# Retention: a head's group statistics used one chunk later, and its transposes released head by head

## What is computed

```python
def head_groupnorm(o):                       # over the 512 channels of a head
    mu = jnp.mean(o, axis=-1, keepdims=True)
    var = jnp.mean(jnp.square(o - mu), axis=-1, keepdims=True)
    return (o - mu) * lax.rsqrt(var + GN_EPS)

q, k, v, z_ret, u_val, u_gate, z_conv, g_a, g_b = jnp.split(h @ w_in, split_at, axis=-1)
ret = head_groupnorm(retention_chunkwise(rotary(q), rotary(k), v))   # 4 heads, 512 value channels each
y_a = (ret * jax.nn.silu(z_ret)) @ w_ret_out

a = u_val * jax.nn.sigmoid(u_gate)
a = causal_depthwise_conv_2(a, conv_w, conv_b)                       # 31 taps, 1024 channels
a = jax.nn.silu(layernorm(a))
y_b = (a * jax.nn.silu(z_conv)) @ w_conv_out
merged = jax.nn.sigmoid(g_a) * y_a + jax.nn.sigmoid(g_b) * y_b
```

## Time and profile before

| | |
|---|---|
| Median of 3 runs | 933.23 us (931.78 to 934.69) |
| Profiled execution | 932.75 us, its span 930.7 us |
| PE busy | 887.7 us |
| DVE busy | 693.0 us |
| ACT busy | 509.9 us |
| POOL busy | 46.1 us |
| HBM read | 156.58 MB |

### The profile page before, as it was taken

How to read it: one execution, slowest core, us unless ns; L and a number is a source line. 1 busy time by engine, 2 the same in 40 slices (tenths; PEclk the granted TensorE clock), 3 DMA queues, 4 the chain that set the end, 5 groups by cost and what they waited for, 6 DMA issues and landing times.

```text
span 930.7 us, 16363 instructions
## 1 busy us (share of the span) xinstructions
PE 887.7 (95%) x6434; PEld 826.9 (89%) x6434; DVE 693.0 (74%) x1116; ACT 509.9 (55%) x728; POOL 46.1 (5%) x48
## 2 busy tenths in 40 slices
PE   5898998989989899999999999999999989999997
PEld 5898997879867899999998889999887779999995
DVE  4676887944765767777777677899998879965874
ACT  4587884645444555556555555433345566445642
POOL 0001120012110000000000000000001130001000
PEclk9899998988999799999999979999999999999999
DMA  7825564540068257777778616555554435654441
GB/s 215 262 88 162 172 191 138 172 96 2 27 217 298 78 192 246 261 250 252 249 244 303 211 57 204 181 182 181 167 175 155 137 121 174 203 183 156 144 153 46
DMA packets 139475, 161.58 MB, mean 174 GB/s; under 512 B 17155, under 2 KB 112283, under 8 KB 139419
## 3 DMA queue, kind: packets, MB, share of 16 engines
q1 hardware_dynamic: 139419, 160.80, 53.2%
HBM read 156.58 MB, written 4.21 MB: 173 GB/s over the span
## 4 chain that ended last, share of the span: by engine, by line
PE 76%; DVE 12%; ACT 7%; issue 2%; DMA 2%; SPq 0%; DVEq 0%; ACTq 0%
PE psum L480 22%; PE psum L482 22%; PE psum L481 22%; DVE w_lo L1374 5%; PE psum L765 3%; DVE cv L1817 2%; ACT w_hi L933 2%; DMA w_raw<-in_sc_w_out_dram 1%; DVE cacc L1523 1%; PE psum L635 1%; ACT junk L966 1%; PE psum L869 1%; PE psum L747 1%; PE psum L647 1%; PE psum L604 1%
## 5 line engine op out<-in xcount | busy, mean ns | idle before, releaser
L1374 DVE TENSOR_TENSOR w_lo<-w_raw,w_hi 128x1024 fp32r<-128x1024 f32 x264 | 321.4, 1241 | 151.0 <-ACT w_hi L933 149.9
L933 ACT ACTIVATE w_hi<-w_raw 128x1024 fp32r<-128x1024 f32 x264 | 274.2, 1057 | 223.3 <-PE psum L482 171.5
L480 PE MATMUL psum<-hT_hi,w_hi 128*128 128x256 f32 x1216 | 349.6, 287 | 4.7 <-DVE w_lo L1374 4.0
L481 PE MATMUL psum<-hT_lo,w_hi 128*128 128x256 f32 x1216 | 346.6, 285 | 0.0
L482 PE MATMUL psum<-hT_hi,w_lo 128*128 128x256 f32 x1216 | 346.5, 285 | 0.0
L480 PEld LDWEIGHTS psum<-hT_hi,w_hi 128*128 128x128 f32 x1216 | 236.3, 194 | 6.2 <-issue 4.3
L481 PEld LDWEIGHTS psum<-hT_lo,w_hi 128*128 128x128 f32 x1216 | 236.2, 194 | 0.3 <-issue 0.2
L482 PEld LDWEIGHTS psum<-hT_hi,w_lo 128*128 128x128 f32 x1216 | 235.9, 194 | 0.0
L1817 DVE SCALAR_TENSOR_TENSOR cv<-aP,par,cv 128x256 f32<-128x256 f32 x240 | 98.5, 479 | 0.0
L480 PE MATMUL psum<-w_hi,hT_hi 128*128 128x512 f32 x224 | 92.7, 414 | 2.3 <-DVE w_lo L1374 2.3
L482 PE MATMUL psum<-w_hi,hT_lo 128*128 128x512 f32 x224 | 88.8, 396 | 0.0
(11 more groups left out here) (283 smaller groups left out, 1073.8 us busy)
## 6 DMA issues: line engine op xcount, KB each, us to landing
w_raw<-in_w_in_dram SPq DMA_DIRECT2D x44, 1024.0 KB, 5.0
w_raw<-in_sc_w_in_dram SPq DMA_DIRECT2D x32, 1024.0 KB, 7.5
w_raw<-in_gdn_w_in_dram SPq DMA_DIRECT2D x24, 1024.0 KB, 5.4
ada<-in_w_ada_dram SPq DMA_DIRECT2D x24, 512.0 KB, 4.7
w_raw<-in_gdn_w_out_dram SPq DMA_DIRECT2D x8, 1024.0 KB, 5.2
w_raw<-in_sc_w_out_dram SPq DMA_DIRECT2D x8, 1024.0 KB, 8.0
w_raw<-in_w_ret_out_dram SPq DMA_DIRECT2D x8, 1024.0 KB, 4.9
w_raw<-in_w_conv_out_dram SPq DMA_DIRECT2D x4, 1024.0 KB, 5.0
```

What stands on the lines that cost most here:

```text
L480: pe.matmul(o, l_hi, r_hi, start=start, stop=False, skip_group_check=True)
L481: pe.matmul(o, l_hi, r_lo, start=False, stop=False, skip_group_check=True)
L933: act.activation(w_hi[j % 2 * 2 + h][:, :, :], raw[slot][:, h * KH2:(h + 1) * KH2, :], ACT.Copy).then_inc(hi_ready, 1)
L1374: return dve.tensor_tensor(o, whole, hi.bitcast(F32), ALU.subtract)
```

## The change

ACT and DVE take the square root, reciprocal and scaling of head h out of the odd chunk 2h + 1 and do them at the next chunk, behind its splits: ACT before that chunk's Silu, DVE before its convolution steps. Head 3's stands in zconv chunk 0. PE's block of transposes for pairs 2c and 2c + 1 stands beside zconv chunk c (before: c + 1), waits only for the products of its own head, and for the sums that are still in the banks it writes. ACT's and DVE's yT_hi and yT_lo move with it; ACT's waits for the product that reads the part of `zr` that it overwrites.

```diff
@@ PE
             def turn_two(c):
                 for kp in (2 * c, 2 * c + 1):
-                    if kp == 0:
-                        pe.wait_ge(rg_ready, NT * RH)
+                    pe.wait_ge(rg_ready, NT * (kp // 2 + 1))
+                    pe.wait_ge(gn_ready, min(kp + 5, NT * RH))
                     if kp >= 4:
                         pe.wait_ge(y_op_ready, 2 * KT + kp - 3)
...
-            phase("zconv", hT_hi, hT_lo, True, beside=lambda c: turn_two(c - 1) if c else None)
-
-            phase("gates", hT_hi, hT_lo, True, beside=lambda c: turn_two(KT // 2 - 1) if c == 0 else None)
+            phase("zconv", hT_hi, hT_lo, True, beside=turn_two)
+            phase("gates", hT_hi, hT_lo, True)
@@ ACT
-            def group_norm(i, j, done):
+            def group_norm(h):
+                act.wait_ge(gn_step, 2 * NT * (h + 1))
+                if h:
+                    act.wait_ge(gn_ready, NT * h)
+                act.activation(grs[:, :], gmv[:, :, 1], ACT.Sqrt, bias=eps_n[:, :]).then_inc(gn_std, 1)
+                act.wait_ge(gn_rec, 2 * (h + 1))
+                for t in range(NT):
+                    n = NT * h + t
+                    if h:
+                        act.wait_ge(rg_ready, n - 1)
+                    act.activation(og[t][:, :], psum[:, 4 + n % 4, :], ACT.Identity, scale=grs[:, t:t + 1], bias=gnm[:, t:t + 1]).then_inc(gn_ready, 1)
+
+            def beside_zret(i, j, done):
+                c = 4 * i + j
+                if c and c % 2 == 0:
+                    group_norm(c // 2 - 1)
                 z_ret(i, j, done)
-                if j % NT == NT - 1:
-                    h = (4 * i + j) // NT
...
             def turned_pairs(i, j, done):
+                if j == 0:
+                    group_norm(RH - 1)
                 z_conv(i, j, done)
-                if j == 1:
-                    act.wait_ge(rg_ready, NT * RH)
-                if j:
-                    split_two(j - 1)
+                split_two(j)
 
             def split_two(q):
                 for kp in (2 * q, 2 * q + 1):
+                    if kp < NT * RH // 2:
+                        act.wait_ge(rg_ready, NT * kp + 1)
                     act.wait_ge(yT_turned, KT + kp + 1)
...
-            def last_pairs(i, j, done):
-                gates(i, j, done)
-                if i == 0 and j == 0:
-                    split_two(KT // 2 - 1)
-            chunks("gates", last_pairs, unroll=True)
+            chunks("gates", gates, unroll=True)
@@ DVE
+            def group_scale(h):
+                dve.wait_ge(gn_std, h + 1)
+                dve.reciprocal(grs[:, :], grs[:, :]).then_inc(gn_rec, 1)
+                dve.wait_ge(gn_rec, 2 * h + 1)
+                dve.scalar_tensor_tensor(out=gnm[:, :], in0=gmv[:, :, 0], scalar=-1.0, in1=grs[:, :], op0=ALU.mult, op1=ALU.mult).then_inc(gn_rec, 1)
+
             def group_norm(i, j, done):
                 n = 4 * i + j
                 h, t = n // NT, n % NT
+                if n and t == 0:
+                    group_scale(h - 1)
                 conv_share(7)
...
-                if t == NT - 1:
-                    dve.wait_ge(gn_std, h + 1)
-                    dve.reciprocal(grs[:, :], grs[:, :]).then_inc(gn_rec, 1)
...
             def turned_pairs(i, j, done):
+                if j == 0:
+                    group_scale(RH - 1)
                 conv_share(5 if j else 8)
-                if j:
-                    split_two(j - 1)
+                split_two(j)
...
                 conv_share(8 if c else 4)
-                if c == 0:
-                    split_two(KT // 2 - 1)
```

More of the change, by code:

```diff
@@ L1245, in _ @@
             z_ret = tokens_out(zr, ACT.Silu)
-            def group_norm(i, j, done):
-                z_ret(i, j, done)
-                if j % NT == NT - 1:
-                    h = (4 * i + j) // NT
[L1251 to L1261, removed]
+            def group_norm(h):
[13 more added lines that the diff above has]
+                    group_norm(c // 2 - 1)
+                z_ret(i, j, done)
+            chunks("zret", beside_zret, unroll=True)
             z_conv = channels_out(zc, ACT.Silu)
             def turned_pairs(i, j, done):
+                if j == 0:
+                    group_norm(RH - 1)
                 z_conv(i, j, done)
-                if j == 1:
-                    act.wait_ge(rg_ready, NT * RH)
-                if j:
-                    split_two(j - 1)
+                split_two(j)
             def split_two(q):
                 for kp in (2 * q, 2 * q + 1):
+                    if kp < NT * RH // 2:
+                        act.wait_ge(rg_ready, NT * kp + 1)
                     act.wait_ge(yT_turned, KT + kp + 1)
@@ L1882, in group_norm @@
                 dve.bn_aggr(gmv[:, t, :], gst[:, t, :]).then_inc(gn_step, 1)
-                if t == NT - 1:
-                    dve.wait_ge(gn_std, h + 1)
-                    dve.reciprocal(grs[:, :], grs[:, :]).then_inc(gn_rec, 1)
-                    dve.wait_ge(gn_rec, 2 * h + 1)
-                    dve.scalar_tensor_tensor(out=gnm[:, :], in0=gmv[:, :, 0], scalar=-1.0, in1=grs[:, :], op0=ALU.mult, op1=ALU.mult).then_inc(gn_rec, 1)
             chunks("zret", group_norm, unroll=True)
             def turned_pairs(i, j, done):
+                if j == 0:
+                    group_scale(RH - 1)
                 conv_share(5 if j else 8)
-                if j:
-                    split_two(j - 1)
+                split_two(j)
             def split_two(q):
```

## The result

The changed kernel takes 926.19 us (median of 6 runs, 923.88 to 928.74) against 933.28 us (6 runs of before): ratio 0.9923, 95% interval 0.9904 to 0.9942, so 5.4 to 9.0 us faster. The profiled execution took 926.39 us, with a span of 924.4.

What follows compares the result with a forecast made beforehand. PE, busy 95% of the span, bounds the kernel; only its stops and low clock can return. 6.4 us less 2.1 gives 4.3 off 932.75, so 928.45, plus 0.5 for the median: 928.9, stated as 928.8; range 926.3 to 931.2.

Steps and rivals of the forecast that it cites:

- What could be won: Zret to first gates chunk: four PE stops cost 4.7 us, the clock's fall 1.7; at most 6.4 us can return.
- The circle of waits undone: Zret: ACT and DVE no longer wait for each other once per head; without holds DVE's period falls from 15.8 to 12.1 us.
- no stop in zret: Sign of being right: PE runs through the retention gate without a stop; three of four stops go.
- A convolution step held like w_lo: DVE convolution steps beside POOL's products are held about 1.1 us each, two per head; DVE's period becomes 14.3 us.
- the first rival: Convolution steps not held by POOL: DVE never falls behind, all 6.4 us come, 926.8 us; chance 0.15.
- One stop of about 2 us stands where four were, and costs 2.1 us: Zconv, third chunk's second half: PE waits for a DVE split ready at 768.4 but wanted at 766.2.
- the 4.3 of the sum: Whole kernel: net gain in us, 6.4 to be won less 2.1 for the stop left.
- The transposes earlier save nothing: Zconv: same 32 transposes, 8 yT_hi and 8 yT_lo, moved forward, so no PE work saved; added PE waits cost nothing.
- the clock did not fall after the stop: Rival: the clock falls in the remaining stop, PE loses 1.7 us more, 930.5 us; chance 0.15.
- the holds were not longer: Rival: holds of 1.3 us each, ten before the zconv split, make the stop 4 us; 930.9 us, chance 0.12.
- nothing was slower: Rival: steps held again behind the next POOL product, ten holds of 1.1 + e; at e = 1.0 938.9 us; chance 0.04.
- The clock: After the 1.91 us stop PE fell from 2.4 to 1.2 GHz for a while, worth 1.7 us.

Runs made afterwards that it cites:

- stats_only: The changed kernel with transposes, yT_hi and yT_lo put back where they were before, only the group statistics a chunk later; ratio to before 0.9925.
- before_again: The kernel before the change, once more with no edit, timed beside itself: 932.88 against 933.26 us.
- pool_twice: The changed kernel with every POOL gate product made twice, the first time into a free buffer; ratio to before 1.0053.

## Why the prediction was right or wrong

- **What could be won**: 6.4 us. The stage without any stop is 127.0 us, so before held 133.4 - 127.0 = 6.4. Right; on one of its terms see the last point.
- **The circle of waits undone; no stop in zret; the clock at 1.0 there**: right. DVE's waits went as said, and its first convolution block starts 14.07 us after the first weighted sum (714.59 - 700.52); from 715.5 and before's 701.48 the forecast had 14.0.
- **A convolution step held like w_lo**: right in kind, and it decided against the first rival. The hold was put at 1.1 us; it is 1.04. DVE's period was put at 14.3 us; it is 14.03 (714.59, 728.62, 742.65).
- **"One stop of about 2 us stands where four were, and costs 2.1 us"**: this is the step that was mis-sized. The stop is at the chunk named, for the split named, but 0.78 us long, and costs 128.1 - 127.0 = 1.1. So 1.0 us more came back than the 4.3 of the sum. DVE was put too late: three periods too long by 0.27 make 0.8 us, and the 8 steps with four holds, put at 7.6, took 763.82 - 756.68 = 7.1. About half of these 1.3 us is the price of the hold, 1.1 in place of 1.04 or less, ten times. The other half is DVE's own work: its period without holds was put at 12.1 and is 14.03 - 2.09 = 11.94. The sum took DVE's waits at their idle time alone. In before, the product that follows the reciprocal (gnm) and the next w_lo start 2.62 us apart, with the wait of 2.46 between them,

```profile
728.05 0.16 DVE L1887 SCALAR_TENSOR_TENSOR gnm<-gmv,grs 128x2 f32<-128x2 f32 x1
730.67 3.19 DVE L1374 TENSOR_TENSOR w_lo<-w_raw,w_hi 128x1024 fp32r<-128x1024 f32 x2 [2.46 <-ACT w_hi L933]
```

and in the changed kernel, without a wait, gnm and the next instruction start 0.08 apart (714.51, 714.59): 2.54 us were lost, not 2.46. All of it adds up because DVE is the late engine over the whole way from 714 to 767.
- **The transposes earlier save nothing and put 1.2 us of yT_lo and a block of 0.8 into the first zconv chunk**: right; stats_only shows 0.3 us lost. That the waits of PE on POOL and ACT cost nothing was right too: L895 has none.
- **A slip that changed nothing**: the time at which PE wants the second zconv chunk's split, 759.8, leaves out that stop's own 1.1 us and the 0.79 of the transposes; with both it is 759.5, and DVE's 756.9 is early all the same.
- **The rivals**: the clock did not fall after the stop (1.00 from 754 to 795); the holds were not longer; nothing was slower.
- **The range**: its lower end was the gain without any stop, 6.4 us, from a median. Between two comparisons of the same pair of kernels the difference of the medians was 7.1 and 5.1 us; of the 7.1 one microsecond is in front of the stage in the two profiles, and where the rest arose is not shown. The stage alone, 5.3 us, would have given 927.9, inside the range: that the time fell 0.1 us outside took the mis-sized stop and the scatter together. The range took in the bounds of the costs and forgot that of the measurement, about 2 us.
- **The clock**: as an account of PE's time the 1.7 us are right. As the price of the fall they are wrong: without the fall PE would have waited instead, as before_again shows below.

## What to carry to other kernels

If two in-order engines wait for each other once per round, move the use of the result one round later, behind the work that the other engine is waiting for; here this gave 5.6 us, and letting the consumers start earlier gave nothing. But look first at what ran in the idle time that goes: there POOL's two products of a head had cost DVE 0.85 us together (w_lo x2 at 3.18 in the earlier trace rows against 2.33 without POOL), and as soon as they met DVE's convolution steps they cost 1.04 us each for 1.3 us of POOL. Where one price stands in a sum ten times, its second digit matters, and so does the 0.1 us that a wait costs beyond its idle.

## What was not expected

- **A fall of the clock can be free.** In before_again PE stopped for 1.95 us at the same place as in before, and the clock did not fall after it. PE then ran ahead at full rate, and its next stop was 2.42 us instead of 0.84. The restart came 764.03 - 701.15 = 62.9 us after the first weighted sum, in before 764.41 - 701.48 = 62.9. DVE set that moment: its w_lo for it starts 60.8 us after the mark in both (761.95 - 701.15 and 762.29 - 701.48). PE at half rate merely filled the wait. Afterwards the clock fell after the longer stop, where PE could less well afford it, and the stage was 0.6 us longer. Why the clock fell after 1.91 us in before and not after 1.95 here is open. The w_lo, the stops and the slices of before_again:

```profile
761.95 4.25 DVE L1374 TENSOR_TENSOR w_lo<-w_raw,w_hi 128x1024 fp32r<-128x1024 f32 x2 [2.46 <-ACT w_hi L933]
```

```profile
748.24 0.50 PE L480 MATMUL psum<-w_hi,hT_hi 128*128 128x512 f32 x1 [1.95 <-DVE w_lo L1374]
764.03 0.58 PE L480 MATMUL psum<-hT_hi,w_hi 128*128 128x256 f32 x1 [2.42 <-DVE w_lo L1374]
```

```profile
750.00:752.00 2.00, 2.00 (x9) 1.31 (x8) 2.00 (x6) 0.64 (x1) 0.00 (x0) 1.00 1.06 369
...
764.00:766.00 2.00, 1.97 (x9) 1.97 (x10) 2.00 (x1) 1.99 (x4) 1.12 (x1) 0.50 0.26 63
```

- **Taking turns.** When instructions of both engines are waiting, the rows read as if the two alternate: two POOL products that took 2.52 us back to back before take 2.88 in the changed kernel, and each of the two convolution steps that were held shows some 1.5 us. In pool_twice four products in a row start 1.40 to 1.44 us apart and hold four steps. The order itself is inferred from these lengths.
- **A tensor_scalar is held too**, with one SBUF tensor as its input: two took 2.76 us beside ln_sum and 0.73 without it.
